# A transformer block with routed experts: the last half-matrix of expert weights is loaded in 32 transfers of 8 partitions instead of 2 transfers of 128

## What is computed

```python
def expert_block(args):
    xb, e = args
    return (jax.nn.silu(xb @ w_g[e]) * (xb @ w_u[e])) @ w_d[e]
# w_g, w_u: [32, 1024, 512]   w_d: [32, 512, 1024]
ys = lax.map(expert_block, (xs, block_expert)).reshape(n_rows, d)
y = jax.ops.segment_sum(ys * row_w[:, None], row_tok, num_segments=t + 1)[:t]
return x + y
```

## Time and profile before

| | |
|---|---|
| median of 3 runs | 706.17 us (705.79 to 708.71) |
| span of the profiled execution | 704.8 us |
| TensorE busy | 588.1 us, 83% |
| HBM read | 245.7 MB, 350 GB/s over the span |
| share of the chain that ended last | PE 55%, DMA 40% |

### The profile page before, as it was taken

The page is one execution under the profiler, slowest core; times in us unless marked ns, Lnnn a source line. Parts: engine busy times, 40 slices in busy tenths (PEclk is TensorE's granted clock), DMA queues, the critical chain, the costliest instruction groups (busy, mean ns, idle before and its releaser), DMA issues.

```text
span 704.8 us, 15485 instructions
## 1 busy us (share of the span) xinstructions
PE 588.1 (83%) x6644; PEld 412.3 (58%) x6644; DVE 300.9 (43%) x628; ACT 191.8 (27%) x338; POOL 29.4 (4%) x58
## 2 busy tenths in 40 slices
PE   8999999999999999996776678755887676778775
PEld 6887899999999885553333334432443333334343
DVE  6476976985475945442222322223222223222232
ACT  5584455463545444111011001110011101011011
POOL 2612000000000020000000000000000000000000
PEclk9999999999999999998787876888679878878799
DMA  9995446436579799999999999999999999999994
GB/s 317 313 349 187 138 136 223 151 140 218 181 276 421 313 375 347 427 426 422 429 427 425 426 428 427 426 425 428 429 423 428 426 425 428 428 428 426 423 419 178
DMA packets 40260, 247.78 MB, mean 352 GB/s; under 512 B 4440, under 2 KB 6624, under 8 KB 26112
## 3 DMA queue, kind: packets, MB, share of 16 engines
q1 hardware_dynamic: 37728, 245.44, 86.4%
q0 software_dynamic: 912, 1.25, 0.9%
q10 hardware_dynamic: 1552, 0.10, 0.2%
HBM read 245.72 MB, written 1.06 MB: 350 GB/s over the span
## 4 chain that ended last, share of the span: by engine, by line
PE 55%; DMA 40%; another core or an unknown queue 2%; DVE 1%; issue 1%; ACT 0%; SPq 0%; DVEq 0%; ACTq 0%
DMA wide<-in_w_expert_up 34%; PE ps L1431 9%; PE ps L1067 7%; PE ps L1068 7%; PE ps L1069 7%; DMA wide<-in_w_expert_down 5%; PE ps L1462 4%; PE ps L1040 3%; PE ps L1042 3%; PE ps L1391 3%; PE ps L1041 3%; PE ps L1505 1%; PE ps L1446 1%; PE ps L1400 1%; DMA x_tok<-in_x 1%
## 5 line engine op out<-in xcount | busy, mean ns | idle before, releaser
L1431 PE MATMUL ps<-wide,xe 128*32 128x256 f32 x2048 | 162.8, 472 | 105.3 <-DMA wide<-in_w_expert_up 104.6
L1431 PEld LDWEIGHTS ps<-wide,xe 128*32 128x32 f32 x2048 | 76.6, 131 | 172.6 <-issue 128.9
L1986 DVE TENSOR_TENSOR xe<-ps,g_ffn 128x256 f32<-128x256 f32 x32 | 13.6, 425 | 256.5 <-PE ps L1400 256.3
L1581 DVE TENSOR_TENSOR ring_lo<-ring,w_hi 128x1024 fp32r<-128x1024 f32 x76 | 91.3, 1221 | 40.9 <-ACT w_hi L748 40.5
L748 ACT ACTIVATE w_hi<-ring 128x1024 fp32r<-128x1024 f32 x76 | 78.9, 1056 | 55.8 <-PE ps L1069 34.9
L1067 PE MATMUL ps<-hT_hi,w_hi 128*128 128x256 f32 x320 | 89.5, 280 | 0.6 <-DVE hT_lo L1597 0.6
L1068 PE MATMUL ps<-hT_lo,w_hi 128*128 128x256 f32 x320 | 88.5, 277 | 0.0
L1069 PE MATMUL ps<-hT_hi,ring_lo 128*128 128x256 f32 x320 | 88.5, 277 | 0.0
L949 ACT ACTIVATE he<-ps 128x128 f32<-128x128 f32 x32 | 8.9, 278 | 203.6 <-PE ps L1446 200.0
L1462 PE MATMUL ps<-wide,he 128*32 128x256 f32 x1008 | 61.2, 382 | 2.7 <-DMA wide<-in_w_expert_down 2.7
L1067 PEld LDWEIGHTS ps<-hT_hi,w_hi 128*128 128x128 f32 x320 | 60.2, 188 | 1.1 <-DVE ring_lo L1581 0.7
(11 more groups left out here) (289 smaller groups left out, 781.0 us busy)
## 6 DMA issues: line engine op xcount, KB each, us to landing
wide<-in_w_expert_gate SPq DMA_DIRECT2D x27, 2048.0 KB, 45.5
wide<-in_w_expert_up SPq DMA_DIRECT2D x27, 2048.0 KB, 48.7
wide<-in_w_expert_down SPq DMA_DIRECT2D x27, 2048.0 KB, 41.1
ring<-in_w_in SPq DMA_DIRECT2D x8, 2048.0 KB, 14.9
ring<-in_w_merge_gate SPq DMA_DIRECT2D x6, 2048.0 KB, 9.7
wide<-in_w_expert_gate SPq DMA_DIRECT2D x10, 1024.0 KB, 9.1
wide<-in_w_expert_up SPq DMA_DIRECT2D x10, 1024.0 KB, 13.4
wide<-in_w_expert_down SPq DMA_DIRECT2D x9, 1024.0 KB, 9.0
```

Source lines behind the costliest of these rows:

```text
L1431: ins = t_.matmul(ps[q * WIN:(q + 1) * WIN, b, 0:QW], xe[b][:, k % 2, k // 2, :], w, start=(k == 0), stop=(k == KD - 1))
L1581: v.tensor_tensor(piece(ring_lo, g, c), piece(ring, g, c), by_row(out_hi[g == 19][c]).bitcast(F32), ALU.subtract).then_inc(wpre_lo, 1)
```

## The change

The two transfers of the last unit become 32: for each column half sixteen of 8 partitions (`LANES`), 2 rows and 512 columns, 32 KB each. The eight partitions of one transfer lie four apart, in one window of 32 partitions. All sixteen of a half raise one semaphore, by 16 each; TensorE waits for 256 of them instead of 16. The second half has a semaphore of its own now instead of the ring place's.

```diff
+LANES = 8
+N_LAST = P // LANES
...
-        last_in = sem("last_in")
+        last_in = [sem(f"last_in{i}") for i in range(len(LAST))]
...
-            return sum(1 for m in range(n % RING, n + 1, RING) if m % 2 == 0 or m not in paired)
+            return sum(1 for m in range(n % RING, n + 1, RING)
+                       if m < UNITS - 1 and (m % 2 == 0 or m not in paired))
...
                 if n == UNITS - 1:
+                    into = unit[j].rearrange("p (k n) -> p k n", n=D)
+                    part = src[e, :, c * UNIT:(c + 1) * UNIT].rearrange("p (k n) -> p k n", n=D)
                     for i, cols_i in enumerate(LAST):
-                        sp.dma_start(unit[j].rearrange("p (k n) -> p k n", n=D)[:, :, cols_i],
-                                     src[e, :, c * UNIT:(c + 1) * UNIT].rearrange("p (k n) -> p k n", n=D)[:, :, cols_i]
-                                     ).then_inc(unit_in[j] if i else last_in, 16)
+                        for at in range(0, P, WIN):
+                            for r in range(WIN // LANES):
+                                eight = slice(at + r, at + WIN, WIN // LANES)
+                                sp.dma_start(into[eight, :, cols_i], part[eight, :, cols_i]).then_inc(last_in[i], 16)
...
                 for i, qs in enumerate(LAST_Q):
-                    if i == 0:
-                        pe.wait_ge(last_in, 16 * p + 16)
-                        u = unit[n % RING]
-                    else:
-                        u = landed_unit(p, n)
+                    pe.wait_ge(last_in[i], (16 * N_LAST) * p + 16 * N_LAST)
+                    u = unit[n % RING]
```

## The result

The change makes the kernel slower: 710.46 us median (710.05 to 710.61) against 705.99 us for the kernel before in the same comparison, a ratio of 1.0057 with a 95% interval of 1.0046 to 1.0067. The forecast was 706.2 us, with a range to 709.6. The profiled execution's span is 708.5 us where it was 704.8.

The account below looks back on a forecast made before the run. The prediction took the DMA weight stream and, at the end, unit 190's landing to bound the kernel. Its terms summed to 0 on the 704.8 us span; with the median 1.4 us above, 706.2 us, range 705.0 to 709.6.

Parts of the forecast that it names:

- What bounds the kernel: Whole kernel: a weight stream at full DMA pace; its end hangs on unit 190's landing at 695.02, not the last unit's.
- Part (2), the spread: Last unit's load: each eight-partition transfer runs on only eight engines, 2.6 us for a half, 5.2 for both.
- which eight: Last unit's load: all transfers on the eight engines ahead, costing 0, or on the eight behind, costing 2.5 us.
- the lagging eight: Rival, last unit's load: all transfers fall on the eight engines behind; +2.5, 708.7 us; chance 0.19.
- unit 190, which every engine carries, still lands at 695.02: Transfer ahead of the last unit: its landing stays put, so the gain is 0 to 0.3 us, taken as 0.
- The sum: Whole kernel: all parts together change the 704.8 us span by 0, giving a median of 706.2 us.
- Part (3), SP's issues: SP's queue at the last unit: 30 more issues at 0.39 us, 12.5 us for 32, taken as costing nothing.
- Part (4), completions: Last unit's load: 32 completions on each of eight engines instead of 2, at most 0.2 us in all.
- The trickle: Rival, last unit's load: small transfers go one in 0.39 us after unit 190; +9.9, 716 us; chance 0.05.
- the pace of the issue: Rival, SP's issues: lagging engines, and the last eleven transfers wait for SP; +3.9, 710.1 us; chance 0.09.
- the sign that I had named for the pace: End of the DMA stream: a foot of share under 0.5, and SP's issues of the last unit ending after 695.
- Why some engines are behind: DMA engines at the end: instruction fetches, 56 us laid on eight engines, 7 us each, as likely cause.

Follow-up runs that it names:

- probe: The kernel before, with eight tiny transfers of 1 to 8 partitions queued behind the last unit; one execution, 708.9 us.
- all_lower: The changed kernel, all 32 small transfers writing partitions 0 to 63, the upper rows into an unused ring place; 708.97 us, ratio 1.0035.
- upper_only: The changed kernel with only the sixteen small transfers to partitions 64 to 127, the other half of the unit not loaded; 710.48 us, ratio 1.0060.
- lower_only: The changed kernel with only the sixteen small transfers to partitions 0 to 63, the other half of the unit not loaded; 706.38 us, ratio 0.9999.
- sixteen: The changed kernel with sixteen transfers of 16 partitions, eight apart, instead of 32 of 8 partitions; 710.61 us, ratio 1.0054.
- split64: The kernel before, with each column half of the last unit in two transfers of 64 partitions instead of one of 128; 710.58 us, ratio 1.0056.
- contig_lower: As lower_only, but each small transfer takes eight neighbouring partitions instead of eight that lie four apart; 708.85 us, ratio 1.0039.

## Why the prediction was wrong

**What bounds the kernel.** Right for the kernel before: nothing moved ahead of the last units, and its end hangs on unit 190's landing. In the changed kernel it hangs on both. From unit 190 at 696.97 and at the low clock TensorE comes to the last combination at 702.34; the last small transfer at 701.05 would hold it until 702.08 by the estimate above.

**Part (2), the spread: eight engines.** Right, and shown by the probe.

**Part (2), which eight.** This is the first step that failed. From the share of 0.52 I read two groups of eight, and let all the transfers fall on one or the other. The windows show how many engines are still busy and not which; the first eight were six ahead and two behind. For the end, two behind are as bad as eight. all_lower gives this case by itself at +2.5 us, which is what I had put on the rival "the lagging eight", by the same sum: its second half is waited for until 700.55, I had written 700.2. The rival had a chance of 0.19 where it deserved more: the forecast needed all eight engines to be ahead.

**Part (2), "unit 190, which every engine carries, still lands at 695.02".** This is the second step that failed. I had costed the moved rows by bytes and engines, and gave no reason why a transfer already in the queue should keep its pace while others write beside it. Load alone, by all_lower's ratio, is 706 x 1.0035 = 708.5 us and within the range, which went to 709.6; crossing is what upper_only has beside lower_only, and what the change has beside all_lower. Unit 190 landed 1.95 us late in the changed kernel, 2.2 us late in upper_only (697.23), 3.6 in sixteen, 5.4 in the slowest execution of split64, and on time in lower_only and all_lower. No rival of mine had it.

**The sum.** The two terms don't add, since the end waits for the later of two landings. Load alone costs 2.5 us (all_lower), crossing with half of the transfers 4.2 (upper_only), the change 4.0 by its ratio. The difference between the change and all_lower, 1.0057 against 1.0035, is at the edge of their intervals (1.0046 to 1.0067 and 1.0020 to 1.0050); what crossing adds on top of the load is therefore known only roughly, about 1.5 us. In the profiles the last small transfer lands at 701.05 here and at 700.51 in all_lower. Crossing delays the small transfers too: the last of sixteen lands at 699.42 in upper_only and at 696.71 in lower_only.

**Part (3), SP's issues.** Mis-sized: 677 ns each instead of 390, 32.6 us from the first to the last instead of 12.5 after the hold. It cost nothing that I could find: the last issue ends at 697.25, and the slowest engine still has a backlog then. From 695 us on its increments come every 0.20 to 0.21 us without a gap, up to the last at 701.05, while issues come every 0.72. The fast engines' last pieces land 1.4 us after that issue, by 698.7. An issue costs 677 ns where the eight rows lie four apart; contig_lower's shortest, with eight neighbours, is 301 ns.

**Part (4), completions.** Mis-sized: bounded at 0.2 us in all; by the estimate from all_lower it is 0.04 us for each transfer on an engine, 1.3 us for 32. The bound leaned on the halves of the kernel before, which have one completion for sixteen runs, and says little about one for two.

**The trickle** and **the pace of the issue** did not happen, though the sign that I had named for the pace, issues that end after 695, is there: it does not tell the two apart.

**Why some engines are behind.** No run moved the instruction fetches, so the cause is not shown, but the trace of the kernel before speaks for them. From one transfer to the next the sixteen landings either keep their distances or grow apart by one step of about 1.5 us, at times up to 2.5: 35 such steps between 282 and 690 us, and 34 fetches of 16 KB, each about 1.07 us long, in the same stretch. What was wrong is that they fall on one half of the engines; the probe shows engines behind among the first eight too.

## What to carry to other kernels

When a transfer is cut across the partitions, ask of every engine which rows it now writes and which it wrote before: here cuts into 64 partitions, into 16 that lie eight apart, and into 8 of the upper half slowed down the transfers in flight, by up to half, and a packet's duration by size, or GB/s for each 1.00 of DMA share, shows it at a glance. The same 8-partition transfers to the lower half, four rows apart, did not. A cut along the columns, with all 128 partitions in every transfer, has neither this cost (309 and 84 ns in the kernel before) nor the uneven load, and it was already there.

A unit that the diff doesn't touch can be what gets late. Where a forecast says "this one stays where it is", it needs a reason of its own.

## What the runs showed of the hardware that I had not expected

- Sixteen DMA engines that carry equal bytes drift apart: in the kernel before one transfer's landings spread over 2.0 us at 282 us and over 9.1 us at the end (688.45 to 697.59), and a transfer ends when the slowest engine does. In the probe's run the first eight engines stand at 688.6, 689.2, 690.5, 690.8, 692.1, 693.3, 695.0 and 696.2 us.
- A transfer of n partitions, n from 1 to 8, runs on n engines, those of the shorter transfers among them.
- While transfers on the first eight engines write partitions 64 to 127 beside transfers of 128 partitions, packets of 8 KB take 590 ns instead of 309 and packets of 2 KB 164 instead of 84 (upper_only against lower_only, 688 to 692 us).
- A transfer of eight rows four apart costs SP 677 ns to issue, where the output's, over all partitions, take 390, and an engine an estimated 0.04 us beyond its data.
- The granted clock at the end is 1.00 in some executions and 0.50 in others of nearly the same program, and the way from unit 190's landing to the end of the span takes 12.8 us at 0.50 (lower_only) where it takes 9.8 at 1.00.
